# One low part moved to POOL, and splits and turns of the norm output placed elsewhere in the queues

## The chip, the cores and the metric

The kernel runs on one core of one Trainium2 chip. The metric is the device time of one execution in microseconds. Engine names: PE is TensorE (PEld its weight loads), DVE is VectorE, ACT is ScalarE, POOL is GpSimd, SP issues the transfers.

## What is computed

Two transformer blocks on 256 tokens of 1024 values, all in float32. The first block mixes a sparse attention (compressed, selected and window branches) with a retention, then a gated feed-forward layer with a short convolution; the second has two layers of differential attention, a 31-tap convolution and a Fourier branch, and again a feed-forward layer. What matters for the change is the start of the first block, and the norm ahead of each layer of the second:

```python
h = rms_norm(x, norm_mix_w[layer])
proj = h @ w_in[layer]
q_nsa, kv_nsa, g_nsa, q_ret, k_ret, v_ret, g_ret, g_merge = jnp.split(proj, split_at, axis=-1)
...
kc = compress(k_cmp, pe_k, w1_k, w2_k)      # gelu(blk @ w1) @ w2
vc = compress(v_cmp, pe_v, w1_v, w2_v)
s_cmp = jnp.einsum('bshgd,bchd->bhgsc', qg, kc).astype(jnp.float32) * scale
p_cmp = masked_softmax(s_cmp, mask_cmp)
...
scores = jnp.einsum('bnihd,bnjhd->bnhij', qc, kc) * decay_in    # retention
o_inner = jnp.einsum('bnhij,bnjhe->bnihe', scores, vc)
...
h = rmsnorm(x, norm1_g[l])                   # second block, layers 0 and 1
u = h @ w_in[l]                              # k, q, v, ...
```

## The kernel before

**Products.** Each float32 product is made of three products of rounded values: a matrix is split into a high part (rounded to fp32r) and a low part (the remainder), and hi*hi, hi*lo and lo*hi are added up in PSUM. The weights come as chunks of 128 x 2048 values, numbered in the order of `PLAN`. For each chunk SP loads `raw`, ScalarE copies it to `whi` (line 1048), and then one engine subtracts to get `wlo`, in the same memory as `raw`: VectorE in one instruction (line 1670), or, if the chunk is in `POOL_LO`, GpSimd in four quarters of 128 x 512 (line 1551). There are 6 `raw` and 4 `whi` buffers. A high part needs the `whi` buffer of the chunk four before, which TensorE must have finished.

**Order.** Nothing is scheduled by the machine: each engine has its own program, a queue in an order written by hand, and takes its instructions strictly in that order, with waits on semaphores between the engines. `splits(n)` makes all parts up to chunk n that are not made yet; VectorE passes over those in `POOL_LO`. `rows(u)` and `feats(u)` are the products of one unit of weights. On ScalarE and VectorE they make the splits ahead of time, at the "take" of a chunk: `splits(i + AHEAD)` with `AHEAD` 3. `steps(g, n)` advances such a unit by n steps, and the first step runs its take:

```python
for what, i, _, _, tt in rows_steps(u):
    if what == "take":
        splits(i + ahead)
    elif what == "out" and out:
        out(tt)
    elif what == "step":
        yield
```

`weave(front, back, n)` puts n steps of the units in `back` behind each yield of `front`, in every engine's program.

**Chunks that the change touches.** `cmpk` is 8 and 9, `cmpv` 10 and 11 (the weights of the two compressions), `kr` 12 and 13, `vr0` 14 and 15, `vr1` 16 and 17, `gm0` 22 and so on to `gm5`, 27.

**The first block around the change.** TensorE makes `cmpk` and `cmpv`, turns (transposes) `kT`, then makes the first step of `kr`, turns `Hs` (the output of the gelu), a second step, the products of `Hg` (VectorE's copy of the turned `Hs`) that give the compressed keys (line 672), a third step, the products of `Hr` (VectorE's copies at 1905) that give the compressed values, and the rest of `kr`. Then `nsa()` is woven with `vr0`, `vr1`, `sg0`, `sg1`, `gm0`, `gm1`: first the scores of the compressed part (line 691), two steps of `vr0`, and the turning of `cp` (line 696), which VectorE makes from these scores by masking, maximum, exponent on ScalarE, sum and scaling (lines 1925 to 1944). After `nsa()` the heads `oaT` are turned and split, and `retention()` is woven with `gm2` to `gm7`, three steps at a time. Per head, VectorE multiplies the scores by the decay to `STt` (line 2040), and makes the statistics of the head before (lines 2029 to 2033); on ScalarE `retention()` begins with one Silu over `sg` (line 1282), and POOL multiplies `sg` by `gnw` when the Silu is done (line 1567).

**The second block around the change.** The norm ahead of layer 0 is called `n3`, that ahead of layer 1 `n5`. `norm_turned(norm, tt, halves)` turns the scaled rows of the token half `tt` on TensorE, 4 blocks of 128 for each of the two column halves; ScalarE makes the high part and VectorE the low part (`hhi`, `hlo`, lines 1097 and 1707). For `tt` 0 this happens in the last products of the feed-forward layer. In VectorE's program the low parts of both halves are followed by the additions of the feed-forward output to `x` for `tt` 1 (lines 2097 and 1746), and then by `splits(q0)`. In `layer()` the groups `part(n, ks, tt)` use the chunks k0, k1, q0, q1 (n 0 to 3); n 0 and 2 use column half 0, n 1 and 3 half 1.

Of the kernel before, what the change touches and what calls it, by code (L numbers as in the profile page):

```python
# [22 lines left out]
NRAW, NHI, AHEAD = 6, 4, 3  # L23
# [59 lines left out]
GATES = (8, 9, 10, 11, 0, 1, 2, 3, 4, 5, 6, 7)  # L83
# [116 lines left out]
def steps(g, n):  # L200
    for _ in range(n):
        next(g, None)
# [66 lines left out]
PLAN, UNITS = chunk_plan()  # L269
# [1 line left out]

POOL_LO = {i for l in range(2) for u in (*(f"g{l}_{f}" for f in GATES[1:]), f"pc{l}_0", f"pc{l}_1") for i in UNITS[u]}
POOL_LO |= {UNITS[f"{w}{l}"][1] for w in "kq" for l in range(2)}
POOL_LO |= {i for f in range(3, NFT, 2) for i in UNITS[f"up0_{f}"]}

# [221 lines left out]
def pe_program(pe, t, ev, pb):  # L499
# [83 lines left out]
    def norm_turned(norm, tt, halves=(0, 1)):  # L583
        for h in halves:
            turned(("xT", norm, tt, h), [("xn", norm, tt, h)], t.xn[tt][:, half(h)], 4,
                   None if norm == "n0" else 4 + 2 * tt + h)
# [29 lines left out]
    g = rows("kv2", *h)  # L616
# [13 lines left out]
    g = rows("qr", *h)  # L630
# [220 lines left out]
    def ffn(n, norm, after):  # L851
        ev.name("pe_turned", ("up starts", n, "pe"))
        for f in range(NFT):
            g = feats(f"up{n}_{f}", *h, 8, of_norm_feats(norm))
            if f == 0:
                steps(g, 2)
                x_turned(norm, 1, 1)
            if f == 1:
                steps(g, 4)
                late_row(norm)  # L860
            run(g)
        banks = {}

        def down(i, k, kg, tt, hf, ends=()):
            pe.wait_ge(*on("lo", i))
            pe.wait_ge(*on("g", n, kg))
            wh, wl = weights(i, t.whi[i % NHI]), weights(i, t.wlo[i % NRAW])
            if kg == 0:
                banks[tt, hf] = fixed_bank((f"dn{n}", tt, hf), 4 + 2 * tt + hf)
            ends = list(ends) + ([("got", f"dn{n}", tt, hf)] if kg == NFT - 1 else [])  # L870
            mul3(t.ps[banks[tt, hf]][:, :], t.ghi[:, kg, tok(tt)], t.glo[:, kg, tok(tt)], wh[:, k, half(hf)],
                 wl[:, k, half(hf)], kg == 0, kg == NFT - 1, ends)

        chunks = UNITS[f"dn{n}"]
        def part(c, k, tt, hf):
            i = chunks[c]
            down(i, k, 2 * c + k, tt, hf, [("used", i)] if k + tt + hf == 3 else [])

        held = 3 if after else 2
        for c in range(len(chunks) - held):  # L880
            for k in range(2):
                for tt in range(2):
                    for hf in range(2):
                        part(c, k, tt, hf)
        last = [(c, k) for c in range(len(chunks) - held, len(chunks)) for k in range(2)]
        if after:
            for tt in range(2):
                for c, k in last:
                    if tt and (c, k) == last[-1 if after == "n3" else -2]:
                        norm_turned(after, 0)  # L890
                    for hf in range(2):
                        part(c, k, tt, hf)
            return
        for tt in range(2):
            for hf in range(2):
                for c, k in last:
                    part(c, k, tt, hf)
# [4 lines left out]
    def layer(l, norm):  # L902
# [3 lines left out]
                       4 + tt + 2 * (w == "k"))  # L906

        part = part_of((f"k{l}", f"q{l}"), *h, lambda kg, tt: ("h", norm, tt, kg // 4))
        part(0, range(4), 0)
        part(1, range(4), 0)  # L910
        early = 3 if norm == "n3" else 2
        part(2, range(early), 0)
        norm_turned(norm, 1, (0,))
        part(2, range(early, 4), 0)
        part(0, range(2), 1)
        norm_turned(norm, 1, (1,))
        part(0, range(2, 4), 1)
# [104 lines left out]
def act_program(act, t, ev, pb):  # L1022
# [16 lines left out]
    def splits(last):  # L1039

        while upto[0] <= min(last, len(PLAN) - 1):
            i = upto[0]
            upto[0] += 1
            act.wait_ge(*on("raw", i))
            if i >= NHI:
                act.wait_ge(*on("used", i - NHI))
            n = width(i)
            act.op.activation(t.whi[i % NHI][:, 0:n], t.raw[i % NRAW][:, 0:n], ACT.Copy).then_inc(  # L1048
                *at("act_hi", ("hi", i)))
# [221 lines left out]
        *[feats(f"gm{f}", 8, gate_out(f, [("kr", "rot", 0), ("kr", "rot", 1)])) for f in range(2)],  # L1271
    )
    weave(nsa(), back, 2)
    splits(UNITS["gm2"][0] + AHEAD)
    heads_upper("oaT", 4, t.oah)


# [243 lines left out]
def pool_program(pool, t, ev, pb):  # L1521
# [34 lines left out]
    for tt in range(2):  # L1556
        norm_power("n0", tt)
    for w in ("qr", "kr"):
        for tt in range(2):
            a = t.ra[2 * (w == "kr") + tt]  # L1560
            pool.wait_ge(*on("free", (w, tt)))
            pool.op.tensor_tensor(a[:, :], a[:, :], t.rb[tt][:, :], ALU.add).then_inc(
                *at("pool_small", (w, "rot", tt)))
# [73 lines left out]
def dve_program(dve, t, ev, pb):  # L1637
# [4 lines left out]
    def bank(name):  # L1642
        return t.ps[pb.find(name)]
# [16 lines left out]
    def splits(last):  # L1660

        while upto[0] <= min(last, len(PLAN) - 1):
            i = upto[0]
            upto[0] += 1
            if i in POOL_LO:
                continue
            dve.wait_ge(*on("raw", i))
            dve.wait_ge(*on("hi", i))
            c = slice(0, width(i))
            dve.op.tensor_tensor(t.wlo[i % NRAW][:, c], t.raw[i % NRAW][:, c], t.whi[i % NHI][:, c].bitcast(F32),  # L1670
                                 ALU.subtract).then_inc(*at("dve_lo", ("lo", i)))

    def rows(u, out=None, ahead=AHEAD):
        for what, i, _, _, tt in rows_steps(u):
            if what == "take":
                splits(i + ahead)
            elif what == "out" and out:
                out(tt)
            elif what == "step":
                yield  # L1680
# [28 lines left out]
    def copied(names, dst, src, *after):  # L1709
        for w in after:  # L1710
            dve.wait_ge(*on(*w))
        dve.op.tensor_copy(dst, src).then_inc(*at("dve_out", *names))

    def value_out(u, dst, after):

        def out(tt):
            if tt == 0:
                copied([("free", (u, 0))], dst, bank((u, 0))[:, 0:dst.shape[-1]], ("got", u, 0), *after)
        return out
# [174 lines left out]
    for tt in range(2):  # L1894
        copied([("free", ("kT", tt))], t.kT[:, :, tok(tt)],
               bank(("kT", tt))[:, 0:256].rearrange("p (k s) -> p k s", k=2), ("kT", tt))
    kr = UNITS["kr"]
    g = rows("kr", rotated("kr"), 1)
    copied([("Hg",), ("free", ("Hs",))], t.Hg[:, :, :, 0:30],
           bank(("Hs",))[:, 0:128].rearrange("p (v h c) -> p v h c", v=2, h=2)[:, :, :, 0:30], ("Hs",))  # L1900
    copied([("kcT",)], t.kcT[:, 0:15], t.sc[1][:, 0:15], ("kc",))
    splits(kr[1])
    await_own("dve_out")
    for hf in range(2):
        dve.op.tensor_copy(t.Hr[:, hf, :].rearrange("p (g r c) -> p g r c", g=2, r=4),
# [86 lines left out]
    def nsa():  # L1992
# [11 lines left out]

    qr_read, kr_read = ([(w, "T", tt) for tt in range(2)] for w in ("qr", "kr"))
    back = chain(
        rows("vr0", value_out("vr0", t.vr[0][:, 0:512], qr_read), 2),
        rows("vr1", value_out("vr1", t.vr[0][:, 512:1024], qr_read)),
        rows("sg0", value_out("sg0", t.sg[:, 0, 0:512], kr_read)),
        rows("sg1", value_out("sg1", t.sg[:, 0, 512:1024], kr_read)),  # L2010
        *[feats(f"gm{f}", 8) for f in range(2)],
    )
    weave(nsa(), back, 2)
    splits(UNITS["gm2"][0] + AHEAD)
    heads_lower("oaT", 4, t.oal, t.oah)
    ev.name("dve_out", ("nsa ends", "dve"))

# [508 lines left out]
```

## Time and profile before

| | us |
|---|---|
| median of 3 runs | 1308.57 |
| lowest and highest run | 1307.16, 1308.6 |
| time of the profiled execution | 1308.6 |
| its span in the trace | 1307.2 |
| TensorE busy | 1290.0 |
| VectorE busy | 859.5 |
| ScalarE busy | 667.1 |
| POOL busy | 354.7 |

The 1.4 us between time and span lie around the traced instructions. Times in the views are microseconds from the start of the span. A busy TensorE is not necessarily at its peak clock; the granted clock is a column of its own, where 1.00 is 2.4 GHz and the other level is 1.2 GHz.

### The profile page before, as it was taken

Reading aid. Unit: us, or ns where it says so; the run is one execution under the profiler, and the core shown is the slowest. Engines: PE = TensorE matmul, PEld = TensorE weight load, DVE = VectorE, ACT = ScalarE, POOL = GpSimd, SP = SyncE. Lnnn points to the kernel's source line nnn. Section 1 sums busy time; section 2 is a strip of 40 time slices with the busy share of each in tenths; the row PEclk is TensorE's granted clock in tenths of the full one; section 3 lists DMA queues with packets and bytes.
Section 4 is the critical chain, followed back from the end, with each engine's and each line's share of the span. In section 5 each row is a group of like instructions: output and inputs, shape, how many; then the busy total and the mean of one; then the engine's idle time right before and its main releaser. Section 6 shows DMA issues by size and latency. Waiting matters only on the chain.

```text
span 1307.2 us, 21308 instructions
## 1 busy us (share of the span) xinstructions
PE 1290.0 (99%) x8888; PEld 1190.5 (91%) x8888; DVE 859.5 (66%) x1261; ACT 667.1 (51%) x941; POOL 354.7 (27%) x262
## 2 busy tenths in 40 slices
PE   7999999999999999999999999999999999999998
PEld 6978899989999879799999999888989999999987
DVE  6765556668888468896467666536888466766642
ACT  6634444556655355476745444435456674544431
POOL 0110011005441049466450000007847633000000
PEclk9999999999999999999999999999999999999999
DMA  9743324455545546733454555544853444555550
GB/s 346 252 157 129 130 81 155 168 186 185 193 171 186 194 152 246 234 130 130 161 195 177 185 173 191 194 161 165 280 188 130 158 148 178 187 172 190 189 191 40
DMA packets 36143, 231.22 MB, mean 177 GB/s; under 512 B 4432, under 2 KB 4816, under 8 KB 10064
## 3 DMA queue, kind: packets, MB, share of 16 engines
q1 hardware_dynamic: 36048, 229.87, 49.6%
q8 instruction: 70, 1.15, 0.4%
q14 instruction: 25, 0.20, 0.1%
HBM read 222.52 MB, written 1.05 MB: 171 GB/s over the span
## 4 chain that ended last, share of the span: by engine, by line
PE 96%; DVE 2%; ACT 1%; POOL 1%; DMA 1%; issue 0%; POOLq 0%; DVEq 0%; SPq 0%
PE ps L575 18%; PE ps L577 18%; PE ps L576 18%; PE ps L516 11%; PE ps L518 11%; PE ps L517 11%; PE ps L521 7%; PE ps L535 2%; DVE wlo L1670 1%; PE ps L960 1%; PE ps L725 0%; POOL sg L1567 0%; DMA x<-in_x 0%; DVE hlo L1794 0%; DMA gnw<-in_rows 0%
## 5 line engine op out<-in xcount | busy, mean ns | idle before, releaser
L1048 ACT ACTIVATE whi<-raw 128x2048 fp32r<-128x2048 f32 x205 | 390.4, 1908 | 304.6 <-PE ps L577 199.9
L1670 DVE TENSOR_TENSOR wlo<-raw,whi 128x2048 fp32r<-128x2048 f32 (+1 forms) x165 | 380.6, 2311 | 176.5 <-ACT whi L1048 175.6
L575 PE MATMUL ps<-hhi,whi 128*128 128x256 f32 x1696 | 483.3, 285 | 0.0
L577 PE MATMUL ps<-hhi,wlo 128*128 128x256 f32 x1696 | 479.8, 283 | 0.0
L576 PE MATMUL ps<-hlo,whi 128*128 128x256 f32 x1696 | 479.8, 283 | 0.0
L576 PEld LDWEIGHTS ps<-hlo,whi 128*128 128x128 f32 x1696 | 325.2, 192 | 0.6 <-issue 0.2
L575 PEld LDWEIGHTS ps<-hhi,whi 128*128 128x128 f32 x1696 | 325.1, 192 | 0.7 <-issue 0.2
L577 PEld LDWEIGHTS ps<-hhi,wlo 128*128 128x128 f32 x1696 | 325.2, 192 | 0.0
L1551 POOL TENSOR_TENSOR wlo<-raw,whi 128x512 fp32r<-128x512 f32 x160 | 203.7, 1306 | 142.3 <-ACT whi L1048 139.3
L1529 POOL TENSOR_TENSOR st<-st,sm 128x1 f32<-128x1 f32 (+2 forms) x28 | 48.1, 1717 | 407.5 <-DVE st L1723 315.1
L516 PE MATMUL ps<-whi,hhi 128*128 128x512 f32 (+1 forms) x272 | 110.0, 405 | 1.6 <-DVE hlo L1782 0.9
L517 PE MATMUL ps<-wlo,hhi 128*128 128x512 f32 (+1 forms) x272 | 106.1, 390 | 0.0
L518 PE MATMUL ps<-whi,hlo 128*128 128x512 f32 (+1 forms) x272 | 106.1, 390 | 0.0
L516 PE MATMUL ps<-whi,ghi 128*128 128x512 f32 x264 | 102.9, 390 | 0.0
L517 PE MATMUL ps<-wlo,ghi 128*128 128x512 f32 x264 | 102.7, 389 | 0.0
L518 PE MATMUL ps<-whi,glo 128*128 128x512 f32 x264 | 102.7, 389 | 0.0
L2240 DVE SCALAR_TENSOR_TENSOR ps<-gp,sm,ps 128x256 f32<-128x256 f32 x232 | 99.3, 483 | 0.0
L516 PEld LDWEIGHTS ps<-whi,hhi 128*128 128x128 f32 x272 | 52.1, 192 | 14.3 <-DVE hlo L1707 2.5
L518 PEld LDWEIGHTS ps<-whi,hlo 128*128 128x128 f32 x272 | 52.1, 191 | 10.7
L517 PEld LDWEIGHTS ps<-wlo,hhi 128*128 128x128 f32 x272 | 52.3, 192 | 9.4 <-issue 0.2
L518 PEld LDWEIGHTS ps<-whi,glo 128*128 128x128 f32 x264 | 49.6, 188 | 10.3
L517 PEld LDWEIGHTS ps<-wlo,ghi 128*128 128x128 f32 x264 | 49.6, 188 | 10.2
(290 smaller groups left out, 1806.6 us busy)
## 6 DMA issues: line engine op xcount, KB each, us to landing
raw<-in_w SPq DMA_DIRECT2D x203, 1024.0 KB, 4.8
raw<-in_w SPq DMA_DIRECT2D x8, 256.0 KB, 6.2
kst<-kh SPq DMA_DIRECT2D x16, 128.0 KB, 3.1
qst<-qh SPq DMA_DIRECT2D x16, 128.0 KB, 2.3
raw<-in_w SPq DMA_DIRECT2D x2, 560.0 KB, 14.3
x<-in_x SPq DMA_DIRECT2D x2, 512.0 KB, 5.0
gain<-in_rows SPq DMA_DIRECT2D x2, 512.0 KB, 9.3
csT<-in_cs SPq DMA_DIRECT2D x2, 512.0 KB, 3.8
```

Of the source, the lines that this page charges most:

```text
L516: pe.op.matmul(o, sh, mh, start=start, stop=False, skip_group_check=True)
L517: pe.op.matmul(o, sh, ml, start=False, stop=False, skip_group_check=True)
L518: signalled(pe.op.matmul(o, sl, mh, start=False, stop=stop, skip_group_check=True), names)
L521: signalled(pe.op.matmul(o, a, b, start=start, stop=stop, skip_group_check=True), names, "pe_small")
L575: pe.op.matmul(o, wh[:, k, c:c + 128], hi[:, k, :], start=first, stop=False, skip_group_check=True)
L576: pe.op.matmul(o, wh[:, k, c:c + 128], lo[:, k, :], start=False, stop=False, skip_group_check=True)
L577: ins = pe.op.matmul(o, wl[:, k, c:c + 128], hi[:, k, :], start=False, stop=last, skip_group_check=True)
L1048: act.op.activation(t.whi[i % NHI][:, 0:n], t.raw[i % NRAW][:, 0:n], ACT.Copy).then_inc(*at("act_hi", ("hi", i)))
L1529: pool.op.tensor_tensor(o, a, small(t, "mhalf")[:, 0:a.shape[-1]], ALU.pow).then_inc(*at("pool_small", name))
L1551: pool.op.tensor_tensor(t.wlo[i % NRAW][:, half(k)], t.raw[i % NRAW][:, half(k)], t.whi[i % NHI][:, half(k)].bitcast(F32), ALU.subtract).t ...
L1670: dve.op.tensor_tensor(t.wlo[i % NRAW][:, c], t.raw[i % NRAW][:, c], t.whi[i % NHI][:, c].bitcast(F32), ALU.subtract).then_inc(*at("dve_lo ...
L2240: ins = dve.op.scalar_tensor_tensor(t.cv[:, f, :] if j == 30 else acc, t.gp[:, f, j:j + S], cw[:, f, j:j + 1], acc, ALU.mult, ALU.add)
```

## The change

Five edits in the programs of the engines. The products, their operands and the transfers stay the same.

1. Chunk 14 (the first of `vr0`) joins `POOL_LO`: POOL makes its low part, after its sums for `qr` and before those for `kr`.
2. VectorE's splits around `kr` go in another order: the splits up to 14 come directly behind the copies of `kT`, `kr` splits three chunks ahead instead of one, with its first step in front of the copy of `Hg` and a step behind each of the next two copies; `vr0` splits three chunks ahead instead of two.
3. ScalarE and VectorE no longer call `splits(UNITS["gm2"][0] + AHEAD)` (chunk 27) between `nsa()` and the split of `oaT`. The take of `gm2` makes the same call, behind the first part of `retention()`.
4. For `n3`, only column half 0 of the first token half is turned in the feed-forward layer; half 1 is turned behind the first two steps of k0 in layer 0.
5. In layer 1, three steps of q0 instead of two stand before the turning of the second token half.

```diff
-POOL_LO = {i for l in range(2) for u in (*(f"g{l}_{f}" for f in GATES[1:]), f"pc{l}_0", f"pc{l}_1") for i in UNITS[u]}
+POOL_LO = {UNITS["vr0"][0]}
+POOL_LO |= {i for l in range(2) for u in (*(f"g{l}_{f}" for f in GATES[1:]), f"pc{l}_0", f"pc{l}_1") for i in UNITS[u]}
@@ TensorE, ffn()
-                        norm_turned(after, 0)
+                        norm_turned(after, 0, (0,) if after == "n3" else (0, 1))
@@ TensorE, layer()
-        part(0, range(4), 0)
+        part(0, range(2), 0)
+        if norm == "n3":
+            norm_turned(norm, 0, (1,))
+        part(0, range(2, 4), 0)
         part(1, range(4), 0)
-        early = 3 if norm == "n3" else 2
-        part(2, range(early), 0)
+        part(2, range(3), 0)
         norm_turned(norm, 1, (0,))
-        part(2, range(early, 4), 0)
+        part(2, range(3, 4), 0)
@@ ScalarE
     weave(nsa(), back, 2)
-    splits(UNITS["gm2"][0] + AHEAD)
     heads_upper("oaT", 4, t.oah)
@@ POOL
     for w in ("qr", "kr"):
+        if w == "kr":
+            split(UNITS["vr0"][0])
         for tt in range(2):
@@ VectorE
-    def rows(u, out=None, ahead=AHEAD):
+    def rows(u, out=None):
         for what, i, _, _, tt in rows_steps(u):
             if what == "take":
-                splits(i + ahead)
+                splits(i + AHEAD)
@@ VectorE, behind the copies of kT
-    kr = UNITS["kr"]
-    g = rows("kr", rotated("kr"), 1)
+    for i in UNITS["cmpv"]:
+        splits(i + AHEAD)
+    g = rows("kr", rotated("kr"))
+    steps(g, 1)
     copied([("Hg",), ("free", ("Hs",))], t.Hg[:, :, :, 0:30],
            bank(("Hs",))[:, 0:128].rearrange("p (v h c) -> p v h c", v=2, h=2)[:, :, :, 0:30], ("Hs",))
+    steps(g, 1)
     copied([("kcT",)], t.kcT[:, 0:15], t.sc[1][:, 0:15], ("kc",))
-    splits(kr[1])
+    steps(g, 1)
     await_own("dve_out")
@@ VectorE
-        rows("vr0", value_out("vr0", t.vr[0][:, 0:512], qr_read), 2),
+        rows("vr0", value_out("vr0", t.vr[0][:, 0:512], qr_read)),
@@ VectorE
     weave(nsa(), back, 2)
-    splits(UNITS["gm2"][0] + AHEAD)
     heads_lower("oaT", 4, t.oal, t.oah)
```

## Rows read from the trace of the kernel before

**Rows 1.** The page: busy us (share of the span) of each engine.
```profile
PE 1290.0 (99%) x8888; PEld 1190.5 (91%) x8888; DVE 859.5 (66%) x1261; ACT 667.1 (51%) x941; POOL 354.7 (27%) x262
```

**Rows 2.** TensorE's waits: who waited for whom, us, times, longest.
```profile
PE ps L696 <- DVE cp L1944: 2.0, 1, 2.0
PE ps L521 <- DVE Hr L1905: 1.1, 1, 1.1
```

**Rows 3.** Timeline, TensorE: start, us, instructions [idle before <- releaser].
```profile
70.87 0.42 PE L521 MATMUL ps<-Hg,sm 128*64 128x15 f32 x8
...
74.04 0.63 PE L521 MATMUL ps<-sm,Hr 128*120 128x64 f32 x4 [1.15 <-DVE Hr L1905]
...
84.22 1.53 PE L521 MATMUL ps<-kcT,qT 64*128 64x15 f32 x16
...
90.66 0.43 PE L696 MATMUL ps<-sm,cp 128*120 128x128 f32 x1 [1.96 <-DVE cp L1944]
```

**Rows 4.** Windows: stretch, length, busy us of each engine, granted clock (PEclk).
```profile
70.00:75.00 5.00, 3.85 (x25) 2.71 (x24) 2.93 (x5) 0.00 (x0) 0.00 (x0) 1.00 0.25 103
...
90.00:95.00 5.00, 4.34 (x13) 3.50 (x14) 3.05 (x5) 1.46 (x1) 0.00 (x0) 0.66 0.52 203
```

**Rows 5.** Timeline, VectorE, 66 to 92 us.
```profile
67.43 0.76 DVE L1712 COPY kT<-ps 128x256 f32<-128x256 f32 x2 [3.92 <-PE ps L658]
69.41 0.28 DVE L1712 COPY Hg<-ps 128x120 f32<-128x120 f32 x1 [1.22 <-PE ps L665]
...
71.44 2.28 DVE L1670 TENSOR_TENSOR wlo<-raw,whi 128x2048 fp32r<-128x2048 f32 x1
...
82.88 5.56 DVE L1670 TENSOR_TENSOR wlo<-raw,whi 128x2048 fp32r<-128x2048 f32 x2
```

**Rows 6.** Timeline, ScalarE: the high part of chunk 14.
```profile
65.52 1.90 ACT L1048 ACTIVATE whi<-raw 128x2048 fp32r<-128x2048 f32 x1
```

**Rows 7.** Timeline, POOL: the second sum for `kr`.
```profile
83.04 3.24 POOL L1562 TENSOR_TENSOR ra<-ra,rb 128x512 f32<-128x512 f32 x1 [1.43 <-DVE rb L1887]
```

**Rows 8.** POOL's quarters by line: duration ns min/median/max, first and last start.
```profile
L1551 POOL TENSOR_TENSOR wlo<-raw,whi x160: 1267/1294/1729, 292.0 to 1048.5; 128x512 fp32r<-128x512 f32 x160
```

**Rows 9.** Timeline, 186 to 201 us, of ScalarE, POOL, VectorE and TensorE.
```profile
186.69 1.91 ACT L1282 ACTIVATE sg<-sg 128x2048 f32<-128x2048 f32 x1
...
189.77 4.75 POOL L1567 TENSOR_TENSOR sg<-sg,gnw 128x1024 f32<-128x1024 f32 x2 [103.49 <-DMA gnw<-in_rows]
...
188.34 0.43 DVE L2029 BATCH_NORM_STATS2 st<-ps 128x6 f32<-128x256 f32 x1 [1.65 <-PE ps L521]
...
189.63 0.55 DVE L2040 TENSOR_TENSOR STt<-ps,dec 128x384 f32<-128x384 f32 x1
...
193.10 1.46 PE L521 MATMUL ps<-vr,STt 128*128 128x256 f32 x6
...
200.07 1.56 PE L521 MATMUL ps<-vr,STt 128*128 128x256 f32 x6 [0.55 <-DVE STt L2040]
```

**Rows 10.** Timeline, 471 to 480 us, of TensorE and VectorE.
```profile
471.35 1.03 PE L535 MATMUL ps<-sm,xn 128*128 128x128 f32 x8
...
479.21 0.50 PE L516 MATMUL ps<-whi,hhi 128*128 128x512 f32 x1
...
472.61 1.29 DVE L1707 TENSOR_TENSOR hlo<-ps,hhi 128x512 fp32r<-128x512 f32 x2 [1.19 <-ACT hhi L1097]
473.81 0.68 DVE L2097 TENSOR_TENSOR x<-ps,x 128x512 f32<-128x512 f32 x1
...
476.87 2.28 DVE L1670 TENSOR_TENSOR wlo<-raw,whi 128x2048 fp32r<-128x2048 f32 x1
```

**Rows 11.** Timeline, TensorE, 896 to 900 us.
```profile
896.34 0.60 PE L535 MATMUL ps<-sm,xn 128*128 128x128 f32 x4
...
898.35 0.50 PE L516 MATMUL ps<-whi,hhi 128*128 128x512 f32 x1
...
899.84 0.60 PE L535 MATMUL ps<-sm,xn 128*128 128x128 f32 x4
```

## The prediction

> **What bounds the kernel now.** I read the shares of the page first: TensorE is busy for 1290.0 of 1307.2 us [rows 1]. So only two things can move the time: idle time of TensorE and the clock that it is granted. No transfer or elementwise work counts unless TensorE waits for it. The reader should therefore look next at who TensorE waited for [rows 2]: 2.0 us on VectorE's `cp` and 1.1 on `Hr`, each once; a third wait, 0.55 on `STt`, is at 200.07 [rows 9]. The timeline of TensorE puts the first two at 90.66 and 74.04 us [rows 3]. The windows give the clock: 0.66 of full between 90 and 95 us, and 1.00 between 70 and 75. With levels of 2.4 and 1.2 GHz, a mean of 0.66 over 5 us is 3.4 us at the lower level, which costs 1.7 us of work [rows 4]. It follows on the 1.96 us wait; the 1.15 us wait brought none. All that the edits can take away lies there: 1.15 + 1.96 + 1.7 = 4.8 us. The rest of the reading is the order of each engine's queue around the five edits: whatever stands ahead of an instruction that TensorE needs is a possible new wait.
>
> **Part 1, chunks 13 to 18 (the edits in `vr0`, `kr`, `cmpv`).** Today VectorE copies `kT`, then `Hg` (69.41), then splits chunk 13 (71.44), which delays `Hr`; later it makes two splits in a row, 82.88 to 88.44, and the masking of the compressed scores, whose products TensorE had started at 84.22, begins only after them: the 1.96 us wait [rows 3, 5]. The change lets POOL make the low part of chunk 14, and moves the splits of 13 and 15 in front of `Hg`: `steps(g, 1)` runs the "take" of `kr`, and with it `splits(15)`, before the copy.
> VectorE leaves `kT` at about 68.1 [rows 5]. ScalarE has finished the high part of 14 at 67.42 [rows 6], so POOL starts then; a quarter takes it 1.29 [rows 8]. The two engines hinder each other: POOL's sum of as many columns as a quarter takes 3.24 when it starts 0.16 after a split of VectorE, and that pair of splits takes 5.56, where one takes 2.28 (I count 2.2, since an instruction starts some 0.08 before the record of the last one ends) [rows 5, 7]. That is taking turns: POOL waits for the first split, the second waits for POOL. Applied here: POOL 67.5 to 68.75, split 13 to 70.95, POOL to 72.2, split 15 to 74.4, `Hg` 0.28, TensorE at 74.7. Today it starts these products at 70.87 [rows 3]. New wait: 3.7 us idle. `Hr` is then ready in time (its wait, 1.15, goes), and the pair of splits is spread: behind the end of `kr` stands only the split of 17, with 1.9 for its high part and 2.2 for itself [rows 5, 6]. The scores are there 4.3 behind that end (two steps of 1.4 and 1.5 for themselves, [rows 3]), so masking starts at about +4.3, or +4.7 if a sum of POOL comes between; `cp` takes 2.2 (88.44 to 90.66), and TensorE has two steps of 1.4 to fill. So 1.96 becomes at most 0.2. Sum of waits: 3.7 - 1.15 - 1.76 = +0.8. The slow stretch of 1.7 us moves from behind the old wait to behind the new and longer one: 0. POOL finishes chunk 14 at about 77, or 79.5 if a further split goes between; it is needed when `vr0` starts, two steps before the scores (84.22 - 2.8), plus the 2.5 of new delay: 84; so POOL's own work (4 x 1.29 = 5.2 us) costs TensorE nothing, and neither do its two sums for `kr` behind it: `kr` is turned only after the compressed part, past 91 us [rows 3]. Bounds: if the engines did not exclude each other, splits end at 72.6, and the wait is 2.0 in place of 3.7.
> No row shows a subtraction of POOL meeting a long split of VectorE: 160 quarters lie between 1.27 and 1.73 us [rows 8]; only the sum of rows 7 does, and I take the turns from it. The Trainium skill, page SBUF — State Buffer, section "Who interferes with whom", says that a VectorE instruction with two SBUF inputs and a GpSimd instruction that reads SBUF exclude each other, and that the order of issue, not the kind of operation, decides who waits. By that rule the wait is 3.7, without it 2.0; rows 7 agree with it.
>
> **Part 2, the removed `splits(gm2 + AHEAD)`.** Chunk 27 is split ahead of `oaT` today, in time in which ScalarE and VectorE are idle. Without the line it is split at the "take" of `gm2`: on ScalarE behind the Silu, which ends at 188.6, so its high part is there at 190.5; on VectorE between `STt` of head 0 and the statistics of head 0, which start at 188.34 today. VectorE's queue stands still until the split is done. POOL starts its product on `sg` at 189.77, 2.37 each; by turns the split runs from 192.15 to 194.35. From the start of the statistics to the end of the next `STt` it takes 1.84 (188.34 to 190.18): 196.2. TensorE wants it at 193.10 [rows 9]: wait 3.1. The later wait of 0.5 at 200.07 then goes. +2.6 us, and a slow stretch of 1.7, since of the two waits of rows 3 the one of 1.96 is the nearer. Bound from below: no exclusion, 190.5 + 2.2 + 1.84 = 194.55, wait 1.4, no slow stretch: +0.9. Nothing is gained in exchange: `oah` waits for TensorE, not for ScalarE's split.
>
> **Part 3, `n3` turned in two parts.** TensorE turns both halves at 471.35 and starts `q0` at 479.21 without a real wait [rows 10]. Turning half 1 after two steps of `k0` puts it at 474.8. From a turn to TensorE's next use takes 2.0 (896.34 to 898.35, [rows 11]): 476.85, where `k1` needs it; that alone costs some 0.3 to 0.5. But VectorE's queue has the low part of half 1 ahead of the additions to x, and these ahead of the split of `q0`. Today the additions start at 473.81 and the split at 476.87. Now they start at 476.7 (two low parts of 0.7 are apart, not in a row); the four instructions take at least 4 x 0.68, so the split starts at 479.4 and ends at 481.6. TensorE is there at 479.21 + 0.5 = 479.7 [rows 10]. Wait 2.0, and everything is 2.5 later than 479.21. The mean for the other half of the tokens, POOL's root, the scaling and POOL's split of `q1` keep their distance to that split, so they add nothing. A wait of 2.0 is as long as the one that brought a slow stretch, and two of the three runs shown lie at 1308.6 and one 1.4 lower, nearly one such stretch; I count half of it, 0.9. Bounds: 2.0 and 4.2.
>
> **Part 4, `early` 3 in place of 2 for `n5`.** The turn at 896.34 moves behind three more products. Six of them take 1.5 us (898.35 to 899.84), so three take 0.7; what follows needs the chain of 2.0 us behind the turn, and has no room to spare [rows 11]. All of it shows: +0.7.
>
> **The sum**, against the profiled execution's own 1308.6 us, which is the median of the runs (1308.57): 0.8 + 2.6 + 1.7 + 2.5 + 0.9 + 0.7 = +9.2, so 1317.8 us, slower by 0.7%.
>
> **The rivals.**
> (a) Not slower: VectorE and POOL run side by side when POOL subtracts. For it: the 160 quarters that never show a long wait; against it: rows 7. Place: splits 13 and 15, and the split of chunk 27. The new waits shrink to 2.0 and 1.4 (-1.7, -1.7), and with them the stretch behind the second (-1.7); if the clock also stays up at `Hg` and at `q0` (-1.7, -0.9), +1.5 is left: 1310.1 us. It decides only if the whole exclusion is absent and no slow stretch follows on the wait at `Hg`; with that one stretch the time is 1311.8, slower again.
> (b) Faster: the copy of `Hg` is not held up, because splits 13 and 15 are over when TensorE needs it, and the later parts stay hidden: -4.8, 1303.8 us. They would have to end by 70.6, and two splits of 2.2 cannot start before 68.1; only an order of VectorE's queue other than I read would do it.
> (c) The clock stays low for two such stretches behind the 3.7 us wait, and for a whole one at `q0`: +1.7 + 0.8, 1320.3 us. The trace has no wait of this length, so nothing speaks against it but that the one stretch it shows was 3.4 us.
> (d) Chunk 14's low part comes too late because POOL loses every turn. It has 84 - 77 = 7 us to spare, three further splits of 2.3; a fourth costs TensorE that much: 1320.1 us.
>
> **How the numbers follow.** Forecast with its own spread (the sum and its halves of a stretch, 1314 to 1319.5): 0.65. (a) 0.12, (b) 0.04, (c) 0.14, (d) 0.05. The range takes the forecast and (c), and goes down to the sum with the lower bounds of all parts and no stretch but the moved one, 0.8 - 1.7 + 0.9 + 2.0 + 0.7 = +2.7: 1311.3 to 1320.5 us. A difference of 0.2%, 2.6 us, is about what a measurement of this kernel can tell from no change; 1311.2 is the border. Half of (a) ends inside it, some of the partial cases too: faster 0.05, same 0.09, slower 0.86.
>
> **What the profile after would show.** Right: TensorE waits once for the copy into `Hg` for 3 to 4 us, once for `STt` near 196 us for about 3, once for a low part near 482 us for 2; no wait for `cp` above 0.5; at least two stretches at the lower clock; POOL's four quarters between 67 and 80 us with two of them stretched to 3.3 us. Wrong: VectorE copying `Hg` before 71 us, the statistics of head 0 still at 188.3 from the same origin, or a split of `q0` that starts within 1 us of its old place.

## The result, and the profile after

The changed kernel takes 1318.97 us (median of 4 runs, 1318.0 to 1320.22); the kernel before, run beside it, takes 1308.59 (4 runs). The ratio is 1.0077, with an interval of 1.0064 to 1.0089: slower by 10.1 us. Forecast were 1317.8 us and +9.2. The profiled execution took 1318.65 us, with a span of 1317.3.

The span is 10.1 us longer, and the page shows how it divides: TensorE is busy for 3.2 us more [rows 1] with the same 8888 instructions, which is the clock; the other 6.9 are waits.

```profile
PE 1293.2 (98%) x8888; PEld 1192.7 (91%) x8888; DVE 860.3 (65%) x1260; ACT 666.9 (51%) x941; POOL 361.8 (27%) x266
```

TensorE's waits (for whom, us in total, times, longest). `cp` and `Hr` are gone [rows 2]. `STt` has grown from 0.55 [rows 9], `Hg` and `wlo` are new, and one of the two waits for `hlo` is new: 3.7 + 3.6 + 1.8 + 0.7, less the 1.96 and 1.15 that went, are 6.7 of the 6.9 us.

```profile
PE ps L522 <- DVE STt L2046: 4.2, 1, 4.2
PE ps L522 <- DVE Hg L1716: 3.6, 1, 3.6
PE ps L517 <- DVE wlo L1674: 1.8, 1, 1.8
PE ps L517 <- DVE hlo L1711: 1.4, 2, 0.7
```

**Part 1.** The timeline of the changed kernel for VectorE, POOL and TensorE (start, us, instructions, idle before):

```profile
67.50 0.76 DVE L1716 COPY kT<-ps 128x256 f32<-128x256 f32 x2 [3.92 <-PE ps L659]
68.18 6.18 DVE L1674 TENSOR_TENSOR wlo<-raw,whi 128x2048 fp32r<-128x2048 f32 x2
74.28 0.27 DVE L1716 COPY Hg<-ps 128x120 f32<-128x120 f32 x1
...
75.49 1.43 DVE L1912 COPY Hr<-Hg 128x120 f32<-128x120 f32 x2
...
83.23 2.29 DVE L1674 TENSOR_TENSOR wlo<-raw,whi 128x2048 fp32r<-128x2048 f32 x1 [3.71 <-ACT whi L1051]
...
67.63 9.07 POOL L1553 TENSOR_TENSOR wlo<-raw,whi 128x512 fp32r<-128x512 f32 x4 [6.20 <-ACT whi L1051]
...
74.60 0.62 PE L522 MATMUL ps<-Hg,sm 128*64 128x15 f32 x8 [3.59 <-DVE Hg L1716]
...
93.79 0.33 PE L697 MATMUL ps<-sm,cp 128*120 128x128 f32 x1
```

Two splits take VectorE 6.18 us, where one takes 2.28 [rows 5], and POOL's four quarters beside them take 9.07, where four take 5.2 [rows 8]. The records one by one show the two engines taking turns. POOL's second quarter starts at 68.90 and is held through the whole first split, and the second split, started at 71.01, is held until that quarter is over:

```profile
68.90 3.31 POOL L1553 TENSOR_TENSOR wlo<-raw,whi 128x512 fp32r<-128x512 f32 x1
71.01 3.35 DVE L1674 TENSOR_TENSOR wlo<-raw,whi 128x2048 fp32r<-128x2048 f32 x1
```

`Hg` is copied at 74.28 in place of 69.41 and TensorE stands idle for 3.59 us. At 93.79 `cp` is in time: its row has no idle time before it. The windows of the changed kernel (columns as in [rows 4]) show what followed the waits:

```profile
70.00:75.00 5.00, 1.41 (x13) 0.90 (x11) 4.55 (x3) 0.00 (x0) 5.00 (x2) 0.87 0.23 95
75.00:80.00 5.00, 5.00 (x19) 4.11 (x18) 2.30 (x4) 0.00 (x0) 1.71 (x2) 0.50 0.00 0
80.00:85.00 5.00, 5.00 (x22) 4.14 (x21) 1.77 (x1) 1.92 (x1) 0.00 (x0) 0.94 0.59 193
...
90.00:95.00 5.00, 4.89 (x28) 3.85 (x27) 3.52 (x10) 1.52 (x2) 0.00 (x0) 1.00 0.20 72
...
200.00:205.00 5.00, 5.00 (x27) 4.65 (x26) 4.54 (x11) 0.00 (x0) 0.70 (x1) 0.66 0.02 3
...
485.00:490.00 5.00, 3.24 (x14) 2.32 (x14) 4.11 (x8) 4.49 (x10) 0.71 (x1) 1.00 0.00 2
```

A mean of 0.87, 0.50 and 0.94 is 1.3 + 5 + 0.6 = 6.9 us at 1.2 GHz, twice the stretch of [rows 4]. It begins before the wait ends at 74.60, and TensorE was working in about 6 us of it, which costs 3.0 us of work. Behind the wait at `STt` one stretch of 3.4 us follows (0.66); behind the wait at `q0`, none (1.00).

**Part 2.** The timeline of ScalarE, POOL, VectorE and TensorE, 188 to 200 us:

```profile
188.25 1.91 ACT L1284 ACTIVATE sg<-sg 128x2048 f32<-128x2048 f32 x1
190.07 1.90 ACT L1051 ACTIVATE whi<-raw 128x2048 fp32r<-128x2048 f32 x1
...
191.72 6.75 POOL L1571 TENSOR_TENSOR sg<-sg,gnw 128x1024 f32<-128x1024 f32 x2 [102.31 <-DMA gnw<-in_rows]
...
192.07 4.21 DVE L1674 TENSOR_TENSOR wlo<-raw,whi 128x2048 fp32r<-128x2048 f32 x1 [3.83 <-ACT whi L1051]
...
197.40 1.10 DVE L2039 TENSOR_SCALAR st<-st 128x2 f32<-128x2 f32 x1
198.42 0.55 DVE L2046 TENSOR_TENSOR STt<-ps,dec 128x384 f32<-128x384 f32 x1
...
199.02 1.97 PE L522 MATMUL ps<-vr,STt 128*128 128x256 f32 x6 [4.21 <-DVE STt L2046]
```

The split of chunk 27 stands ahead of the statistics and takes 4.21 us beside POOL's product (6.75 for two, 4.75 before [rows 9]). A small operation on two values behind it takes 1.10 us, 0.17 where POOL is idle. TensorE waits 4.21 us.

**Part 3.** The timeline of VectorE and TensorE around `q0`:

```profile
482.99 0.69 DVE L1711 TENSOR_TENSOR hlo<-ps,hhi 128x512 fp32r<-128x512 f32 x1 [2.88 <-ACT hhi L1100]
483.60 0.68 DVE L2103 TENSOR_TENSOR x<-ps,x 128x512 f32<-128x512 f32 x1
...
486.25 2.29 DVE L1674 TENSOR_TENSOR wlo<-raw,whi 128x2048 fp32r<-128x2048 f32 x1
...
488.59 0.50 PE L517 MATMUL ps<-whi,hhi 128*128 128x512 f32 x1 [1.76 <-DVE wlo L1674]
```

The low part of half 1 (482.99) and the additions (from 483.60) stand ahead of the split of `q0` (486.25), for which TensorE waits 1.76 us.

### The profile page after: what moved, and what is told of

Its sections match the earlier page's. It is cut to its first block, busy times and chain, and to the rows that moved or that the text cites. A ratio compares the mean times of both kernels' runs of the same rounds, so it can differ in the third digit from the quotient of the medians.

```text
span 1317.3 us, 21310 instructions
## 1 busy us (share of the span) xinstructions
PE 1293.2 (98%) x8888; PEld 1192.7 (91%) x8888; DVE 860.3 (65%) x1260; ACT 666.9 (51%) x941; POOL 361.8 (27%) x266
## 3 DMA queue, kind: packets, MB, share of 16 engines
q8 instruction: 70, 1.15, 0.3%
## 4 chain that ended last, share of the span: by engine, by line
PE 95%; DVE 2%; ACT 1%; issue 0%; DMA 0%; SPq 0%; DVEq 0%; ACTq 0%
PE ps L576 18%; PE ps L578 18%; PE ps L577 18%; PE ps L517 11%; PE ps L519 11%; PE ps L518 11%; PE ps L522 7%; PE ps L536 1%; DVE wlo L1674 1%; PE ps L963 1%; DMA raw<-in_w 0%; PE ps L726 0%; ACT whi L1051 0%; DVE x L2103 0%; DVE hlo L1798 0%
## 5 line engine op out<-in xcount | busy, mean ns | idle before, releaser
L1553 POOL TENSOR_TENSOR wlo<-raw,whi 128x512 fp32r<-128x512 f32 x164 | 212.8, 1329 | 148.5 <-ACT whi L1051 145.4
```

The lines of the kernel that those rows point to most:

```text
L1553: pool.op.tensor_tensor(t.wlo[i % NRAW][:, half(k)], t.raw[i % NRAW][:, half(k)], t.whi[i % NHI][:, half(k)].bitcast(F32), ALU.subtract).t ...
```

## The experiments

The theory: the change costs time at three places, each a wait behind VectorE's queue, and at two of them the wait is doubled because VectorE's split and POOL's instruction take turns; the clock adds a stretch at 1.2 GHz behind some of the waits. The main rival is (a) of the prediction, that the engines do not hinder each other and the order alone costs time. Differences to the kernel before are ratios of runs on the same chip, with their 95% intervals, times 1307.6 us. Where the text compares the medians of two experiments, it says so; some of them ran on different chips.

**The four parts alone.** Each edit alone in the kernel before: `POOL_LO` with all edits around `kr`, `cmpv` and `vr0`; both removed `splits(UNITS["gm2"][0] + AHEAD)`; the two edits for `n3`; `early = 3`.

> Only the first part of the change: chunk 14's low part on POOL, and the splits of chunks 13 and 15 ahead of the copy into Hg. By the trace of the changed kernel (its wait at Hg 3.6 us, no wait at cp, 6.9 us at the lower clock in place of 3.4) the cost is 1.5 us, so 1310.1; the prediction's sum gave +0.8 for it, 1309.4. If the clock behind the wait at Hg stays low for longer when nothing else is changed, it is up to 3 us. If rival (b) held and this part alone freed the path, it would be 1303.8.

> Only the removed splits of chunk 27 ahead of oaT, on both engines. Theory: TensorE waits at 196 us for STt for about 4.2 us in place of the 0.55 later, with one stretch of 3.4 us at the lower clock (1.7 us): +5.3, 1313.9 (the prediction's sum gave +4.3, 1312.9). Rival: the 5.3 us seen between the two traces is an after-effect of part 1, which left the engines in another order here; then this alone is worth about +0.9, the wait of 1.4 without a slow stretch, 1309.5.

> Only n3 turned in two parts. Theory: the additions to x stand ahead of the split of q0, wait of 1.8 us at q0 and 0.7 at its later part, no slow stretch: +2.6, 1311.2. Rival: with a slow stretch behind the wait, as the prediction counted at one half, +4.3, 1312.9. Rival: the wait comes from the changed kernel's later state alone (work carried over from part 2), then +0.5.

> Only early = 3 in place of 2 for n5: the turn is moved behind three more products of 0.25 us, and what follows has no room: +0.7, 1309.3. Rival: VectorE's or ScalarE's queue was the later one there anyway, and the time stays the same, 1308.6.

| | median us | to before, us | interval | forecast in the sum |
|---|---|---|---|---|
| part 1 | 1309.79 | +1.4 | 0.3 to 2.6 | +0.8 |
| part 2 | 1313.16 | +4.4 | 2.9 to 6.0 | +4.3 |
| part 3 | 1310.92 | +2.9 | 1.7 to 4.1 | +3.4 |
| part 4 | 1308.97 | +0.8 | -0.4 to 2.0 | +0.7 |
| sum, and the whole change | | +9.5, +10.1 | | +9.2 |

The parts add up to the whole within their intervals, so no large share of a part's cost is an after-effect of another part. The waits are those of the whole change: 3.6 at `Hg`, 4.1 at `STt`, 1.8 at `q0`. For part 4 the interval holds zero, but the list of waits has what it should cost: two waits for `hlo` of 0.7 each, where the other kernels without this edit have one.

**POOL starts chunk 14 later.** Part 1 with one more wait, so that the quarters do not meet the splits ahead of `Hg`:

```diff
         if w == "kr":
+            pool.wait_ge(*on("Hr"))
             split(UNITS["vr0"][0])
```

> The first part alone, as in the run of part 1, but POOL waits until VectorE has filled Hr before it starts chunk 14; nothing else is moved. If the turns that VectorE and POOL take set the wait at Hg, the two splits ahead of Hg take 4.5 us in place of 6.2, the wait at Hg shrinks from 3.6 to 1.9 us, POOL's four quarters take 5.2 in place of 9.1, and the time is 1.7 us below that of part 1: about 1308.1, or 1306.4 if no slow stretch follows. If two splits take 6.2 us whoever works beside them (rival a), the wait stays at 3.6 and the time is that of part 1, 1309.8.

1306.46 us: 3.3 below part 1 by the medians, 2.9 by the ratios, and 1.4 below the kernel before (interval 0.3 to 2.6 below). The timeline of VectorE and POOL in this run, and TensorE's wait:

```profile
68.22 4.48 DVE L1674 TENSOR_TENSOR wlo<-raw,whi 128x2048 fp32r<-128x2048 f32 x2
...
74.06 5.04 POOL L1552 TENSOR_TENSOR wlo<-raw,whi 128x512 fp32r<-128x512 f32 x4 [12.59 <-DVE Hr L1912]
```

```profile
PE ps L522 <- DVE Hg L1716: 1.9, 1, 1.9
```

Nothing was done but to delay POOL; the splits took 4.48 instead of 6.18, the quarters 5.04 instead of 9.07, the wait 1.9 instead of 3.6. So the turns are real, and together with the slow stretch behind the longer wait they made part 1 a loss. The two profiled executions are 2.7 us apart (1308.8 and 1306.12). Of that 1.7 is the wait at `Hg`, and 1.7 is the clock: it is 1.00 in all windows from 70 to 95 us, where part 1 alone had 3.4 us at the lower level (0.66 between 75 and 80). Other waits of TensorE are 0.7 longer: 0.4 for a later low part (`hlo` at line 1786), 0.2 at `cp`, 0.1 at line 1660. The profiled execution of part 1 is one of its four fastest; the other seven of its 11 runs lie 0.9 to 1.6 us higher, at a mean clock of 0.997 in place of 0.998 to 0.999, which would fit one more stretch.

**POOL's products on `sg` later.** Part 2, with the two products issued behind the small power instructions (the roots) that POOL makes for the statistics of the first two heads:

```diff
+    def sg_gained():
         pool.wait_ge(*on("sg silu"))
         pool.wait_ge(*on("gnw"))
...
     for k in range(4):
...
+        if k == 1:
+            sg_gained()
```

> The second part alone, but POOL's two products on sg are issued behind the roots of the first two retention heads. If the turns between POOL's product and VectorE's split of chunk 27 are the cost, the split takes 2.3 in place of 4.1 us, the small operation on the statistics 0.17 in place of 1.10, and the wait at STt is 1.4 or less in place of 4.1: 1313.2 - 2.7 = 1310.5, and 1308.7 if the slow stretch goes with it. If the place of the split in VectorE's queue alone is the cost, the wait stays above 3.5 and the time at 1313.

The timeline of VectorE, and TensorE's waits:

```profile
190.21 2.29 DVE L1673 TENSOR_TENSOR wlo<-raw,whi 128x2048 fp32r<-128x2048 f32 x1 [3.83 <-ACT whi L1048]
...
193.62 0.17 DVE L2035 TENSOR_SCALAR st<-st 128x2 f32<-128x2 f32 x1
...
201.93 4.35 DVE L1673 TENSOR_TENSOR wlo<-raw,whi 128x2048 fp32r<-128x2048 f32 x1 [1.47 <-ACT whi L1048]
```

```profile
PE ps L521 <- DVE STt L2042: 2.3, 2, 1.3
```

1309.67 us, 3.5 below part 2 by the medians, 3.0 by the ratios, and still 1.4 above the kernel before (0.3 to 2.6). The split of chunk 27 takes 2.29, the small operation 0.17, and the wait of 4.1 us becomes one of 1.3. The meeting has not gone, it has moved: POOL's products now run from 199.40 to 204.13, and a later split, at 201.93, takes 4.35 beside them. The second wait, 1.0 us at 208.08, stands behind that split, two heads after the first wait. The windows from 190 to 205 us have a clock of 1.00. The first wait is the lower bound of the prediction's part 2 (1.4, no exclusion).

**The high part kept early.** Only VectorE's line removed, ScalarE's stays:

```diff
@@ VectorE
     weave(nsa(), back, 2)
-    splits(UNITS["gm2"][0] + AHEAD)
     heads_lower("oaT", 4, t.oal, t.oah)
```

> Of the two removed lines only VectorE's is removed; ScalarE still makes the high part of chunk 27 ahead of oaT. Theory: VectorE would take the split at gm2's take, before the statistics are there, with its high part long ready, so it starts as soon as the take comes and does not meet POOL's product: waits at STt as before (0.6), 1307.7 to 1308.5. Rival: the split lands behind the statistics whatever ScalarE did, since VectorE comes to the take only at 188.3: then it meets POOL's product, the wait at STt is 1.5 to 4 us, and the time is 1310 to 1313.

1308.47 us, ratio 1.0000 (0.9991 to 1.0009): nothing lost, to within 1.2 us. The timeline shows VectorE splitting as soon as it comes to the take, from 186.68 on, and POOL's product starting after that split, at 190.23, when `gnw` has landed:

```profile
186.68 2.28 DVE L1670 TENSOR_TENSOR wlo<-raw,whi 128x2048 fp32r<-128x2048 f32 x1
188.88 0.42 DVE L2028 BATCH_NORM_STATS2 st<-ps 128x6 f32<-128x256 f32 x1
...
190.23 4.73 POOL L1567 TENSOR_TENSOR sg<-sg,gnw 128x1024 f32<-128x1024 f32 x2 [103.86 <-DMA gnw<-in_rows]
```

So the cost of part 2 comes from ScalarE's place: its copy behind the Silu makes VectorE's split of chunk 27 late, and it then meets POOL's product. VectorE's own place alone costs nothing that these runs can tell. POOL's product does not run free here either: the next split, at 193.07, meets it and takes 4.04 us, but TensorE's wait behind it is 0.9, where the kernel before has 0.55.

**The split of `q0` between the additions.** Part 3, with VectorE's split moved:

```diff
             if after == "n3":
                 gained(tt, hf)
+            if after == "n3" and (tt, hf) == (1, 0):
+                splits(UNITS["q0"][0])
@@ layer()
-            splits(q0)
             start_mean(norm, 1)
```

> The third part alone, with VectorE's split of q0 moved between the additions to x for the first and the second half of the columns. Theory (the additions ahead of the split are the cost): the split starts at about 476.5 in place of 477.9 and TensorE's wait at q0 shrinks from 1.8 to 0.4 us; the second half's additions, the mean and the scaling come about 1.5 us later, so part of it returns at the next turn: 1308.5 to 1310.9. Rival (TensorE waits because the high part or its own turn is late): the wait at q0 stays at 1.8 and the time is at 1310.9 or above.

The timeline of VectorE and TensorE:

```profile
477.62 2.28 DVE L1673 TENSOR_TENSOR wlo<-raw,whi 128x2048 fp32r<-128x2048 f32 x1
479.82 0.68 DVE L2100 TENSOR_TENSOR x<-ps,x 128x512 f32<-128x512 f32 x1
...
482.02 0.21 DVE L1758 TENSOR_SCALAR st<-st 128x1 f32<-128x1 f32 x1 [0.79 <-ACT dump L1120]
...
479.96 0.50 PE L516 MATMUL ps<-whi,hhi 128*128 128x512 f32 x1 [0.45 <-DVE wlo L1673]
...
484.27 0.63 PE L535 MATMUL ps<-sm,xn 128*128 128x128 f32 x4 [1.97 <-DVE xn L1742]
```

1312.47 us, +4.8 to before (3.1 to 6.4), 1.6 above part 3 alone by the medians: outside the range given. The wait at `q0` did shrink, from 1.76 to 0.45, so the additions ahead of the split are its cause. But 1.97 came back at the next turn, for `xn`: the mean of the other token half now starts 6.3 us behind the second low part (475.69 to 482.02), where it was 5.5 in part 3 alone (474.62 to 480.08), since it needs the additions. Together the waits are 0.7 longer. The one run with a mean clock of 1.000 took 1310.55, those of part 3 alone 1309.3 to 1309.9, which fits; the rest of the difference is the clock, 0.997 to 0.999 in the other four runs. The one other place that was tried here is thus no better.

**`Hg` first.** Part 1 with the copy into `Hg` put ahead of the splits of 13 and 15 (and the take of `kr`).

> The first part alone, with the copy into Hg put ahead of the splits of 13 and 15. If the splits are in the way and not Hg itself, the wait at Hg goes and the same work delays Hr: wait at Hr of about 3.0 to 3.4 us in place of 3.6 at Hg and 1.1 at Hr before, time 1309 to 1310. If something else delays Hg, its wait stays at 3.6 and the time is that of part 1, 1309.8, or above.

1310.41 us, +2.6 (1.4 to 3.8), above the range given. The wait at `Hg` is gone, and one of 4.0 stands at `Hr`: the splits, not the copy, are in the way, and ahead of `Hr` they cost no less than ahead of `Hg`. It is longer than expected because the copies into `Hr` met POOL as well, 1.21 us in place of 0.35. A later wait, for the `hlo` of line 1785, is 0.9 longer than in part 1 alone.

**The order of the copies.** Parts 2 to 4 left out. POOL makes chunk 14 by the same edits as in the change; VectorE splits 13 while it would wait for `kT`, and `Hg`, `kcT`, `Hr` and `VC` follow at once:

```diff
+    splits(UNITS["kr"][1])
     for tt in range(2):
         copied([("free", ("kT", tt))], t.kT[:, :, tok(tt)], ...
-    kr = UNITS["kr"]
-    g = rows("kr", rotated("kr"), 1)
+    g = rows("kr", rotated("kr"))
     copied([("Hg",), ("free", ("Hs",))], ...
     copied([("kcT",)], t.kcT[:, 0:15], t.sc[1][:, 0:15], ("kc",))
-    splits(kr[1])
...
-        rows("vr0", value_out("vr0", t.vr[0][:, 0:512], qr_read), 2),
+        rows("vr0", value_out("vr0", t.vr[0][:, 0:512], qr_read)),
```

> Edits of the second to fourth part left out. Of the first part: POOL makes chunk 14, the split of 13 is ahead of the copies into kT, and Hg, kcT, Hr and VC follow at once, the split of 15 behind them. If the two waits of the kernel before (1.15 at Hr, 1.96 at cp) and the slow stretch behind the second (1.7) are what can be had, none of them is left and the time is 1303.8 to 1303.0 (before 1307.7 to 1308.6 minus 4.8). Rival: the split of 13 ahead of kT delays kT, TensorE waits there for it or for Hg instead, and the time is that of before or above.

The timeline of VectorE and POOL, and two windows:

```profile
65.04 2.29 DVE L1673 TENSOR_TENSOR wlo<-raw,whi 128x2048 fp32r<-128x2048 f32 x1 [1.73 <-ACT whi L1049]
67.25 0.74 DVE L1715 COPY kT<-ps 128x256 f32<-128x256 f32 x2
69.20 0.28 DVE L1715 COPY Hg<-ps 128x120 f32<-128x120 f32 x1 [1.21 <-PE ps L666]
...
71.35 1.25 DVE L1907 COPY Hr<-Hg 128x120 f32<-128x120 f32 x2
...
73.93 2.28 DVE L1673 TENSOR_TENSOR wlo<-raw,whi 128x2048 fp32r<-128x2048 f32 x1
...
82.30 2.87 DVE L1673 TENSOR_TENSOR wlo<-raw,whi 128x2048 fp32r<-128x2048 f32 x1 [0.64 <-ACT whi L1049]
...
67.36 5.02 POOL L1552 TENSOR_TENSOR wlo<-raw,whi 128x512 fp32r<-128x512 f32 x4 [6.21 <-ACT whi L1049]
```

```profile
70.00:75.00 5.00, 5.00 (x30) 3.67 (x29) 3.10 (x5) 0.18 (x1) 2.38 (x2) 1.00 0.23 95
90.00:95.00 5.00, 5.00 (x25) 3.72 (x23) 2.92 (x3) 0.85 (x2) 0.00 (x0) 1.00 0.29 121
```

1303.91 us (5 runs, 1303.63 to 1304.55), ratio 0.9965 (0.9952 to 0.9977): 4.6 us faster than before by the ratio (3.0 to 6.3), 3.9 by the medians. It is faster than both kernels: the changed one took 1318.97. The gap that VectorE had before `kT` (3.92 idle, [rows 5]) takes the split; `Hg` is copied at 69.20 as before, and no wait for `Hg`, `Hr` or `cp` is in the list. POOL's quarters take 5.02, for no split runs beside them; only `Hr`, 1.25 us for two copies that take 0.35 elsewhere, meets the last quarter.

**The same without POOL.** Chunk 14's low part is VectorE's again.

> As the run with the order of the copies changed (1303.9), but chunk 14's low part is VectorE's again. If POOL's help is what takes away the wait at cp, VectorE has one more split of 2.3 us between Hr and the scores: wait at cp 1 to 2 us, with a slow stretch behind it or without, 1305 to 1307.5. If the order of the copies alone did it, both waits stay away and the time is 1303.9.

1304.61 us (ratio 0.9976, 0.9967 to 0.9985), 0.7 above the run with POOL by the medians and 1.4 by the ratios, whose intervals overlap, with a wait of 0.7 at `cp` and a clock of 1.00 there; both theories expected more or nothing. The order of the copies and splits is worth most of the gain, 3.1 of 4.6 us by the ratios. The move to POOL is worth about the 0.7 us of that wait; the runs do not tell it from nothing with certainty.

**The whole change without the two meetings.**

> The whole change, with the two meetings of POOL and VectorE taken apart: POOL starts chunk 14 when Hr is filled, and its products on sg stand behind the roots of the first two retention heads. Theory: each meeting costs what it cost alone, 3.3 us (1309.8 to 1306.5) and 3.5 us (1313.2 to 1309.7), clock included, and the parts add up: 1319.0 - 6.8 = 1312.2, or, from the four parts' differences, 1307.6 - 1.4 + 1.8 + 3.0 + 0.9 = 1311.9. Rival: in the whole change the savings are lost again at the next wait, because the engines stand in another order there; then 1315 or more.

1312.44 us, ratio 1.0036 (1.0022 to 1.0050): +4.7 in place of +10.1, and as the theory had it, so the two savings add up. Moving the two meetings, with the clock stretches behind the longer waits, is worth 5.4 (by the ratios) to 6.5 us (by the medians) of the 10. As in the run with POOL's products later, the second meeting has moved to a split at 200.81 (4.35 us), with a wait of 1.0 behind it. What is left of the 10 is that and the places in the queues.

## Why the prediction was right, and where its terms were off

For shares of the whole change I take the start of the same instruction in both traces as a landmark: TensorE's first product with `cpT` starts at 95.16 before and 96.71 after; VectorE's `Tm` from scores of the sparse attention at 181.08 and 182.62; the means of `n3` at 467.60 and 474.40 (first token half) and 479.07 and 488.45 (second).

**Part 1, wait at `Hg` 3.7:** measured 3.6; the order POOL, split, POOL, split and its ends were as worked out (two splits over at 74.36 by the rows, 74.4 forecast), and the two quarters in the middle take 3.31 us each, 3.3 forecast. The wait at `cp` shrank to nothing, forecast 0.2. POOL had finished at 76.7, forecast 77, so rival (d) had no place.

**Part 1, the slow stretch just moves (0):** off. It grew from 3.4 to 6.9 us at the lower clock in the profiled run, 3.0 us of work where 1.7 were counted; rival (c) named this. By the landmarks the part costs 1.5 us in the whole change, not 0.8.

**Part 2, wait at `STt` 3.1 - 0.5:** the mechanism held, the size was 4.2 and nothing was left to wait for at the old place. All is 1.54 us later here than in the kernel before (landmark at 181.08). Moved by that, the term had POOL start at 191.3 and the split end at 195.9; POOL started at 191.72, and the split ended 0.4 later, at 196.28. From the statistics to the end of `STt` it took not 1.84 but 2.77, because the small operation, 0.17 in the run where POOL is idle, met POOL too and took 1.10. Less 0.2 by which TensorE itself came later, these 0.4 and 0.9 are the 1.1 by which the wait was longer. The stretch of 1.7 came. In sum 5.3 by the landmarks for 4.3 forecast. Rival (a) is refuted here and at `Hg` by the two runs that delay POOL.

The trace of the kernel before could have settled rival (a) already. The prediction says that no row of it shows a subtraction of POOL meeting a long split of VectorE, and counts the 160 quarters of 1.27 to 1.73 us in the rival's favour. Both are misread. Where a quarter starts first, it keeps its time and the split is the one that is held, so the durations of the quarters alone show nothing. Two splits of the kernel before show it. One starts beside the last of four quarters (292.03 to 297.07), the other beside POOL's second product on `sg`, the very instruction of part 2; each takes 2.28 alone:

```profile
296.05 3.17 DVE L1670 TENSOR_TENSOR wlo<-raw,whi 128x2048 fp32r<-128x2048 f32 x1
...
192.13 2.38 POOL L1567 TENSOR_TENSOR sg<-sg,gnw 128x1024 f32<-128x1024 f32 x1
...
192.98 3.68 DVE L1670 TENSOR_TENSOR wlo<-raw,whi 128x2048 fp32r<-128x2048 f32 x1 [2.81 <-ACT whi L1048]
```

**Part 3, 2.5 + 0.9:** the wait at `q0` was 1.8, forecast 2.0, and everything there is 2.6 later, forecast 2.5. The half stretch did not come in the profiled run. The runs of this part alone are in favour of a half all the same: of 11, four lie at 1309.3 to 1309.9 (mean clock 1.000), four at 1310.7 to 1311.5 (0.999) and three at 1312.5 to 1313.1 (0.997). Read as none, one and two stretches that is 0.9 stretches in the mean, where the kernel before has 0.4 (below): half a stretch more. This reading rests on the times and mean clocks of the runs; no trace shows where in them the stretches lie.

**Part 4, 0.7:** 0.7 by TensorE's new wait for `hlo`, 0.8 alone.

**The sum** of +9.2 against +10.1 is thus in the main two terms that were too small, the stretch behind `Hg` (by 1.3) and the wait at `STt` (by 1.1), and one too large (the half stretch at `q0`, 0.9). These three would make +10.7. Of the 0.6 that is too much, 0.3 is the waits of part 1, which came to 3.6 - 1.15 - 1.96 = 0.5 in place of 0.8; the other 0.3 is what part 1 costs less by the landmarks (1.5) than by its own terms (0.5 + 1.3), and no row explains it. That the total came out near is partly luck: in the profiled run, one error paid for part of the others.

**Rival (b)**, no hold-up at `Hg`, fell for the change as it was made. Its price was about right: the run with the order of the copies took 1303.9 for 1303.8, and reaches it by the only means that the prediction named, another order of VectorE's queue. That the two times agree to 0.1 is luck again: the gain was 3.9 us by the medians, 4.6 by the ratio, against 4.8 counted, because the kernel before beside it took 1307.85 and not 1308.6.

## What to carry to other kernels

Before work is given to a second engine, look up which long instructions of the first it will lie beside: here POOL's four quarters (5.0 us) cost VectorE 1.7 us and TensorE's wait as much when they meet its splits, and nothing when they start 6 us later. Look at both engines' rows for it: the instruction that starts second is the one that is held. And look where a delayed instruction lands: POOL's products on `sg`, moved away from one split, met another. Before an instruction is moved in an in-order queue, ask which instruction that TensorE needs is now behind it; a gap of the engine (3.9 us before `kT`) was the place here that held a whole split at no cost. And price a wait of TensorE of the lengths seen here (1.9 to 4.2 us) with a chance for a stretch at the lower clock, not with a yes or no.

## What the runs showed of the hardware beyond what was expected

**A wait of one length brings a slow stretch in some runs and not in others.** The wait of 2.0 us at `cp` stands in the profiles of seven kernels that have that place unchanged: the granted clock of the window from 90 to 95 us is 0.66 in five and 1.00 in two. The runs of the kernel before show it too: of 85 beside the experiments, 51 lie at 1306.7 to 1307.9 (mean clock 0.999 or 1.000) and 34 at 1308.3 to 1309.8 (0.998 or 0.999), with medians of 1307.1 and 1308.9, about one stretch of 1.7 us apart. The profiled run of before, on which the prediction rests, was of the upper kind. The run with the order of the copies has no wait there, a clock of 1.000 in all its runs, and a spread of 0.9 us. Behind a wait of 1.9 us at `Hg` the profile shows no stretch in one kernel (POOL later) and one of 3.4 us in another (the whole change without the meetings: 0.85 and 0.81 between 70 and 80 us); behind 3.6 us, 3.4 in one and 6.9 in the other; behind 4.0 at `Hr`, 3.4; behind 4.1 and 4.2 at `STt`, 6.9 and 3.4. Behind the 1.8 us at `q0` none of the three profiles that have it shows a stretch. What decides between them no run here shows.

**Some short VectorE instructions are held as long as a split, others not at all.** Beside POOL, an operation on 128 x 2 values that reads and writes SBUF took 1.10 us (0.17 alone), and the pair of copies into `Hr`, also from SBUF, 1.51, 1.43, 1.25 and 1.21 in four kernels (0.35 alone). The two long splits of the first meeting lost 0.6 and 1.1. Copies out of PSUM kept their time beside POOL: 0.17 for `kcT` at 75.28 in the changed kernel, 0.28 for `Hg` at 69.20 in the run with the order of the copies. So did the BATCH_NORM_AGGREGATE on `st` in the changed kernel, 0.18 at 196.66.

**The two engines lose unequally.** In the same meeting of two splits with four quarters, the splits took 1.7 us more than their 4.48 alone, the quarters 4.0 more than their 5.04. The single records say why: each of the two quarters in the middle (3.31, alone 1.3) waited for a whole split, while a split (2.91 and 3.35, alone 2.28) waited only for the rest of a quarter. The Trainium skill, page SBUF — State Buffer, section "Who interferes with whom", has the two engines exclude each other for such operands; the runs that delay POOL agree with it.
